# Feed-forward products of high and low weights: taken by tile instead of by block of sixteen

## The reference, cut to what matters

```python
D_MODEL = 1024; SEQ = 256; DEPTH_2 = 2; D_FF = 2816
def _swiglu(h, wg, wu, wd):
    return (jax.nn.silu(h @ wg) * (h @ wu)) @ wd
...
    for i in range(DEPTH_2):
        h = _rmsnorm(x, ffn1_norm[i])
        x = x + 0.5 * _swiglu(h, ffn1_w_gate[i], ffn1_w_up[i], ffn1_w_down[i])
        h = _rmsnorm(x, mix_norm[i])
        x = x + _mixing(h, positions, w_in[i], w_out[i], fox_forget_bias[i], lbs[i], hgrn_out_norm[i])
        h = _rmsnorm(x, ffn2_norm[i])
        x = x + 0.5 * _swiglu(h, ffn2_w_gate[i], ffn2_w_up[i], ffn2_w_down[i])
    return _rmsnorm(x, final_norm)
```

## Time and profile before

| | |
|---|---|
| median of 3 runs (lowest, highest) | 2231.4 us (2230.72, 2231.51) |
| profiled execution: time, span | 2233.35 us, 2231.6 us |
| PE busy, share of the span | 2116.4 us, 95% |
| PE weight loads busy | 1461.0 us, 65% |
| DVE, ACT busy | 1196.3 us (54%), 765.8 us (34%) |
| second block (about 1195 us to the end) | 1036 us, four feed-forwards from 1207.2, 1531.7, 1718.1 and 2036.7 us |

### The profile page before, as it was taken

How to read it: one execution, slowest core, us unless ns; L and a number is a source line. 1 busy time by engine, 2 the same in 40 slices (tenths; PEclk the granted TensorE clock), 3 DMA queues, 4 the chain that set the end, 5 groups by cost and what they waited for, 6 DMA issues and landing times. The chain is left out here.

```text
span 2231.6 us, 34337 instructions
## 1 busy us (share of the span) xinstructions
PE 2116.4 (95%) x14221; PEld 1461.0 (65%) x14221; DVE 1196.3 (54%) x1883; ACT 765.8 (34%) x1010; POOL 16.9 (1%) x18
## 2 busy tenths in 40 slices
PE   6988999999998999999998999999999999999999
PEld 4857744433334433334436888988888888998888
DVE  4775622222222322223336875888865874888874
ACT  3553311111110101111114554656544653656543
POOL 0000000000000000000000000000000000000000
PEclk9999999999999999999999999999999999999999
DMA  9442789999999999999996655444655655444652
GB/s 374 168 174 120 301 361 429 431 430 430 430 430 430 427 430 430 430 431 430 428 429 216 204 189 189 151 133 134 207 193 180 194 190 193 147 149 135 204 192 76
DMA packets 200265, 625.87 MB, mean 280 GB/s; under 512 B 13201, under 2 KB 150353, under 8 KB 164305
## 3 DMA queue, kind: packets, MB, share of 16 engines
q1 hardware_dynamic: 197536, 622.41, 71.8%
q10 hardware_dynamic: 2608, 1.72, 0.3%
HBM read 623.05 MB, written 1.05 MB: 280 GB/s over the span
## 5 line engine op out<-in xcount | busy, mean ns | idle before, releaser
L2201 DVE TENSOR_TENSOR w_low<-ring,w_high 128x2048 fp32r<-128x2048 f32 x168 | 386.6, 2306 | 169.0 <-ACT w_high L2196 169.0
L2196 ACT ACTIVATE w_high<-ring 128x2048 fp32r<-128x2048 f32 x168 | 320.2, 1910 | 174.3 <-PE bank L2534 139.1
L2529 PE MATMUL bank<-h_both,w_high 128*128 128x512 f32 x1344 | 322.5, 392 | 0.0
L1907 PE MATMUL bank<-ring,ut 128*64 128x512 f32 x1024 | 246.2, 631 | 38.1 <-DMA ring<-in_exp_w_dram 37.9
L2529 PEld LDWEIGHTS bank<-h_both,w_high 128*128 128x128 f32 x1344 | 246.6, 188 | 48.9
L1996 ACT ACTIVATE sg<-glu 128x512 f32<-128x512 f32 x32 | 20.2, 630 | 568.5 <-DVE glu L2069 568.5
L1874 PE MATMUL bank<-ring_odd,xt 128*64 128x512 f32 x960 | 211.4, 598 | 2.3 <-DVE lin L2072 2.3
L1874 PE MATMUL bank<-ring,xt 128*64 128x512 f32 x960 | 209.3, 594 | 0.0
L1907 PEld LDWEIGHTS bank<-ring,ut 128*64 128x64 f32 x1024 | 72.3, 143 | 196.2 <-issue 125.5
L2085 DVE SCALAR_TENSOR_TENSOR xT<-bank,mod,xT 128x256 f32<-128x256 f32 x128 | 54.2, 478 | 223.7 <-PE bank L1918 223.7
L2534 PEld LDWEIGHTS bank<-h_both,w_low 128*128 128x128 f32 x1344 | 167.4, 188 | 7.0
(11 more groups left out here) (569 smaller groups left out, 2788.9 us busy)
## 6 DMA issues: line engine op xcount, KB each, us to landing
ring<-in_exp_w_dram SPq DMA_DIRECT2D x64, 2048.0 KB, 27.9
ring_odd<-in_exp_w_dram SPq DMA_DIRECT2D x64, 2048.0 KB, 28.0
ring<-in_exp_w_dram SPq DMA_DIRECT2D x128, 1024.0 KB, 25.8
ring<-in_ffn_w_gate_dram SPq DMA_DIRECT2D x44, 1024.0 KB, 5.2
ring<-in_ffn_w_up_dram SPq DMA_DIRECT2D x44, 1024.0 KB, 5.2
ring<-in_ffn_w_down_dram SPq DMA_DIRECT2D x44, 1024.0 KB, 4.8
ring<-in_w_in_dram SPq DMA_DIRECT2D x36, 1024.0 KB, 5.3
ring<-in_ada_w_dram SPq DMA_DIRECT2D x24, 1024.0 KB, 12.0
```

The costliest lines, as they stand in the source:

```text
L1907: ins = nc.tensor.matmul(bank[first + dh][at:at + 64, :], ut[:, r % 4, rows:rows + 64], w[:, x, 512 * dh:512 * dh + 512], start=False, sto ...
L2196: nc.scalar.activation(w_bufs[0][u % BUFS], ring2[:, u % RING2, :], ACT.Copy).then_inc(high2, 1)
L2201: nc.vector.tensor_tensor(w_bufs[1][u % BUFS], ring2[:, u % RING2, :], w_bufs[0][u % BUFS].bitcast(F32), ALU.subtract).then_inc(low2, 1)
L2529: return nc.tensor.matmul(b[:, :], w_parts[0][:, at:at + P], moving.rearrange("p a t -> p (a t)"), start=start, stop=False, skip_group_che ...
```

## The change

In the down units and in the gate and up units the low product of a weight tile is issued directly behind the high product of the same tile, and `low2` is waited for ahead of the unit's first product. The count of products, their operands, banks and columns stay as they are. Units 0 and 32 of each feed-forward and the mixing stage are not touched.

```diff
@@ down units
                         order = (4, 5, 6, 7, 0, 1, 2, 3) if g == 0 else range(DC)
                         groups = [order[2 * j:2 * j + 2] for j in range(4)] if g == G - 2 else [order]
+                        pe.wait_ge(low2, u + 1)
                         for j, tiles in enumerate(groups):
                             for i, m in enumerate(tiles):
                                 if g == 0 and i % 4 == 0:
                                     pe.wait_ge(sem(f + "up_taken"), G - 1 + i // 4)
                                 for x in range(2):
                                     high_weights(sums(m), w_parts, D * x + P * m, units[:, 2 * g + x, :, :], g == 0 and x == 0)
-                            if j == 0:
-                                pe.wait_ge(low2, u + 1)
-                            for m in tiles:
-                                for x in range(2):
                                     ins = low_weights(sums(m), w_parts, D * x + P * m, units[:, 2 * g + x, :, :], False)
                             if len(groups) > 1 and j < 3:
                                 ins.then_inc(sem(f + "low_ready"), 1)
@@ gate and up units
                         pe.wait_ge(high2, u + 1)
+                        pe.wait_ge(low2, u + 1)
                         for c in range(DC):
                             for x in range(2):
                                 high_weights(bank_of(mat, g, x), w_parts, T * c + P * x, h_both[:, c, :, :], c == 0)
-                        pe.wait_ge(low2, u + 1)
-                        for c in range(DC):
-                            for x in range(2):
                                 ins = low_weights(bank_of(mat, g, x), w_parts, T * c + P * x, h_both[:, c, :, :], c == DC - 1)
```

## The result

| | before | changed |
|---|---|---|
| median of 4 runs each, us | 2231.06 (2228.01 to 2231.51) | 2249.74 (2248.87 to 2252.51) |
| ratio | | 1.0084 (95% interval 1.0072 to 1.0096) |
| profiled execution, us | 2233.35 | 2249.13 |
| its span, us | 2231.6 | 2247.3 |
| mean granted TensorE clock | 0.984 | 0.986 |

The changed kernel is slower by 18.7 us, 0.84%. The forecast was +6.2 us with a range up to 2245: the direction was right, and the size was a third of what came.

The account below looks back on a forecast made before the run. PE, 95% busy, was taken to bound the kernel by the spacing of its own products. Dearer pairs (+4.2 us) and a new stall (+2.0 us) gave +6.2 us, a median of 2237.6 us from 2231.4, range 2227 to 2245.

Parts of the forecast that it names:

- PE bounds, waits of the other engines cost nothing: Whole kernel: PE is busy 95% of the span, so its own spacing sets the time and other engines' waits cost nothing.
- Term 2: Unit 1 of the second and fourth feed-forward: PE stalls for the low weights, 1.0 us each, +2.0 us.
- The bank costs nothing: Changed units: a low product adding into the bank its high product has just written costs nothing extra.
- Term 1: 1984 high-low pairs of units 1 to 31: each goes from 344.8 to 346.9 ns, 2.1 ns more, +4.2 us.
- All slow: Rival and upper bound for the changed pairs: highs 232.5 plus lows 117.5, 350.0 ns a pair, 2243.7 us; chance 0.12.
- Why 2.1 of the 5.2 ns: Pair price: 2.1 ns more, between runs of four (0.8 ns) and a straight line (4.0 ns); upper bound 5.2 ns.
- Units equal to one another: Profile sign: changed units all 5.55 us apart, in place of two kinds taking turns around 5.52 us.
- Same price: Rival for the changed pairs: a pair keeps its price, total between 2233.4 and 2235.0 us; chance 0.35.
- Fast throughout: Rival for the changed pairs: alternation settles in the fast spacing, 340.6 ns a pair, 2225.1 us; chance 0.13.
- The clock: New unit 1 stall: 1.6 us idle could lower the clock; given no chance of its own, clock row expected as before.

Follow-up runs that it names:

- experiment 1: Kernel before with only the wait for `low2` moved to each unit's front, products still sixteen and sixteen: 2232.65 us against 2231.83, ratio 1.0007.
- experiment 3: Kernel before with high and low products in runs of two, and in runs of eight: 2234.21 us and 2231.78 us, one run each.
- experiment 7: Changed kernel's tile-by-tile order, but three products of 256 columns per tile from unit 3 on: 2234.77 us, one run.
- experiment 4: Kernel before with each 512-column product split into two of 256, three passes of sixteen, units 3 to 31: 2240.97 us against 2232.24, ratio 1.0041.
- experiment 5: 256 columns in three passes from unit 3 on, but unit 3's last tile keeps one product of 512: 2252.42 us, one run.
- experiment 6: Changed kernel with unit 2 of each feed-forward in runs of two: 2249.51 us, one run.
- experiment 8: Tile by tile in 256 columns from unit 3, unit 2 as ten highs, nine lows, six highs, seven lows: 2230.16 us against 2231.37, ratio 0.9999.
- experiment 9: Changed kernel, unit 2 as ten, nine, six, seven; unit 3 begins high high low low: 2249.96 us, ratio 1.0083 to kernel before; without that swap 2247.24 us.
- experiment 10: Changed kernel, unit 2 as ten highs, eight lows, six highs, eight lows, unit 3 beginning high high low low: 2240.92 us against kernel before's 2232.30, ratio 1.0045.
- experiment 2: Kernel before reordered so high and low products alternate one by one, each low belonging to the tile two back: 2246.07 us, one run.
- experiment 11: Tile by tile in 256 columns from unit 3, unit 2 as ten highs, eight lows, six highs, eight lows: 2224.76 us against 2232.30, ratio 0.9969.

## Why the prediction was wrong, point by point

- *PE bounds, waits of the other engines cost nothing.* Right: 95% busy, clock row unchanged, no steady unit waits for `low2`.
- *Term 2, the wait, +2.0 us.* Right, mechanism and size. The idle times in unit 1 were 1.39 and 1.48 us where 1.6 was said, and 3.4 - 1.39 - 1.48 = 0.5 us in the first feed-forward, as said; the 3.4 is all there is. `add_up` did not wait in the second and fourth. Alone it cost 1.7 us in the trace of experiment 1; in the changed kernel the two stretches grew by 2.5 us, unit 1's own dearer pairs included. The total of experiment 1, +0.8 us, does not resolve it.
- *The bank costs nothing.* Right: experiments 3 and 7.
- *Term 1, 1984 pairs x 2.1 ns = +4.2 us.* **This is the step that failed, with its upper bound "All slow".** It measured 8.5 ns a pair, 1984 x 8.5 = +16.9 us, four times the term, and the pair (353.3 ns) lies above the bound of 350.0. With the wait's 1.7 us that is 18.6 of the 18.7 us. The step treated a pair as a high of one kind plus a low of one kind, each with a price that runs show, and so took the dearest run of highs (232.5) and of lows (117.5) for the worst. What experiments 4 to 10 show in its place is that the unit of price is the repeating pattern of the whole sequence: the alternation has highs at 234, 237 and 231 ns (mean 234.0, where the term had 229.4 and the bound 232.5) and lows at 123, 118 and 117 (mean 119.3, for 117.5). In the kernel before, highs of 233 to 236 ns stand only among the first five products of a run, and no low behind or between them is spaced by 120 to 125 ns. A bound added from kinds seen in runs is none for a sequence that the trace does not hold.
- *Why 2.1 of the 5.2 ns.* The reading that runs of four cost 0.8 ns led me to expect little more at one. Experiment 3 shows how weak that was: runs of two cost 0.2 ns and runs of one 8.5. The step from two to one is the whole effect.
- *Units equal to one another.* Right, but at 5.65 us, above the 5.60 of "all slow".
- *The rivals.* "Same price" fell with 353.3 ns. "Fast throughout" as worded, alternation at 340.6 ns, never came. A faster pattern for the alternation does exist, 348.9 ns, and even that lies above the forecast's 346.9. The prediction worked from one gap per count of columns, 215.8 ns at 512, from which a pair costs the same in any order. The section that it cited (the Trainium skill, TensorE: Matmul & The Clock Gate, Back-to-back issue gap) calls this the gap of an isolated product and says that in a stream of weight loads and products both set the spacing, with about 131 ns at 512 columns; of the order of sizes it says nothing. No run here agrees with either figure, since products of 512 columns are spaced by 228.9 ns on average in runs, nor with an order that is free: the same products cost 344.6 to 345.6 ns a pair in runs of two to sixteen and 348.9 or 353.3 taking turns. The measurement decides.
- *The clock.* It did not fall at the new stalls (0.986 against 0.984).

What stays open: which part of TensorE keeps the pattern, and why strict alternation is dearer than runs of two. No experiment measured loads of weights apart from products. Which pace a stretch takes behind a wait differs between the feed-forwards of one execution (experiments 4 and 8), and I can say only what it was in each trace. Experiments 2, 3, 5, 6, 7 and the half without the swap in 9 have one run each, so what they show stands on their traces and not on their times. The mixing stages, which also show both paces of 256-column products, were not tried.

## What to carry to other kernels

Where PE never waits, cost a reordering by the spacing of starts over a whole repeating sequence, not by adding mean times of its products; if the trace does not hold that sequence, the sum has no upper bound from kinds seen elsewhere, and one run of the new sequence is worth more than the sum. Keep two or more products of a kind together rather than one and one when their sizes differ. When a tuned kernel's times spread wide at the same clock, look for a stretch whose spacing is set by what comes before it: here products of one size, entered from the fast kind, gained 0.31%.

## What the runs showed of the hardware

- One and the same sequence of products runs at two paces: 256 columns at 113.3 or 117.8 ns, 256 and 512 in turn at 348.9 or 353.3 ns a pair, with the granted clock at 1.00 at either pace (experiments 4, 8 and 9). Runs of 512 columns repeat 226, 229 and 232 ns.
- A pace holds for hundreds of products up to a whole feed-forward (30 units of 48 in the first of experiment 8). It changed at a wait of PE (0.50 us, experiment 4), at a barrier (1.5 us, experiment 11) and at one product of another size (experiment 5), though not at every wait: the barrier left it in experiments 7 and 8.
- The repeating sums are whole multiples of 6.67 ns: 1060 ns are 159 of them for three pairs, 1046.7 are 157, three products of 256 columns are 51 or 53, and three of 512 are 103. At the fast pace of 256 columns the start times stay within 1 ns of that grid for 130 us (second feed-forward of experiment 7).
- In runs of high products without a disturbance, fast lows followed a last high spaced by 231 or 232 ns, and slow lows one spaced by 225 to 226 or by 229 to 230 ns.
- A kernel's time thus depends on how its stretches were entered: 6.4 us for each feed-forward of experiment 8, as its slow third one shows beside the others. That this also makes its times spread over 18 us from one execution to the next is likely, but only one was traced.
